# Two attention stages issued in another order, and the second rotary table's angles computed by GpSimd

## The reference

```python
# first block, per layer
y_mla  = mla_mixer(u_mla, ...)         # softmax attention, 4 heads, rotary angles of table 1
y_diff = diff_mixer(u_diff, ...)       # difference of two softmaxes, then rms_norm over the head
y_sb   = sb_mixer(u_sb)                # stick-breaking attention
mix = jnp.concatenate([y_mla, y_diff, y_sb], axis=-1) @ w_o[i]
h = layer_norm(DEEPNORM_ALPHA * h + mix, ln1_g[i], ln1_b[i])
# then 16 experts (grouped_moe) and a second layer_norm

# second block, per layer
a = gla_branch(gq, gk, gv, gg, glr, w_gate_up, b_gate, gla_norm_w) @ w_branch[0]
b = gmlp_branch(gz, gmlp_ln_g, gmlp_ln_b, gmlp_w_s, gmlp_b_s) @ w_branch[1]
c = moba_branch(mq, mk, mv, positions) @ w_branch[2]      # rotary angles of table 2
ga, gb, gc = jnp.split(jax.nn.sigmoid(gl), N_BRANCH, axis=-1)
x = layer_norm_2(x * alpha + (ga * a + gb * b + gc * c) @ w_out, ...)
```

## Time and profile before

| | before |
|---|---|
| median of three runs | 1705.57 us |
| the profiled execution, its own time | 1704.55 us |
| span of its instructions in the profile | 1703.3 us |
| PE busy | 1645.7 us (97%) |
| DVE busy | 890.1 us (52%) |
| ACT busy | 716.9 us (42%) |
| POOL busy | 33.0 us (2%) |

### The profile page before, as it was taken

One profiled execution on the slowest core, in us unless ns is written; L12 is line 12 of the kernel. 1 busy time (PEld: TensorE's weight loads), 2 busy tenths in 40 slices (PEclk: granted clock), 3 DMA queues, 4 the chain that ended last, 5 costly groups with the idle time before them and its releaser, 6 DMA issues.

```text
span 1703.3 us, 25713 instructions
## 1 busy us (share of the span) xinstructions
PE 1645.7 (97%) x10980; PEld 1287.6 (76%) x10980; DVE 890.1 (52%) x1174; ACT 716.9 (42%) x1078; POOL 33.0 (2%) x56
## 2 busy tenths in 40 slices
PE   8899999997999999998999999999999999999998
PEld 7778644434978744433989998899889899989997
DVE  7786411113587511113568556655566675675555
ACT  4685211112575311112654543544446454354443
POOL 1000000000000000000001000000000100000000
PEclk9999999999999999998999999999999999999999
DMA  9436999997736999998744555555556355546552
GB/s 282 153 130 219 373 418 416 416 417 267 239 116 223 373 417 416 416 417 311 234 149 149 174 193 178 198 186 185 177 174 198 119 179 168 203 141 230 186 185 75
DMA packets 193111, 413.11 MB, mean 243 GB/s; under 512 B 16416, under 2 KB 130848, under 8 KB 176608
## 3 DMA queue, kind: packets, MB, share of 16 engines
q1 hardware_dynamic: 191904, 409.81, 66.8%
q10 hardware_dynamic: 1088, 1.57, 0.4%
HBM read 409.52 MB, written 1.84 MB: 242 GB/s over the span
## 4 chain that ended last, share of the span: by engine, by line
PE 85%; DVE 8%; DMA 4%; ACT 2%; issue 1%; POOL 0%; SPq 0%; ACTq 0%; DVEq 0%
PE PS L1619 12%; PE PS L488 10%; PE PS L492 10%; PE PS L489 10%; PE PS L496 8%; PE PS L499 8%; PE PS L500 8%; PE PS L1641 6%; DMA arena<-in_w_up 2%; DVE weights_lo L468 2%; PE PS L1653 2%; PE PS L1594 2%; PE PS L515 2%; DMA weights_raw<-in_w_in 1%; DVE hT_lo L705 1%
## 5 line engine op out<-in xcount | busy, mean ns | idle before, releaser
L468 DVE TENSOR_TENSOR weights_lo<-weights_raw,weights_hi 128x1024 fp32r<-128x1024 f32 x368 | 431.1, 1216 | 189.3 <-ACT weights_hi L461 188.8
L461 ACT ACTIVATE weights_hi<-weights_raw 128x1024 fp32r<-128x1024 f32 x368 | 365.5, 1044 | 135.3 <-PE PS L500 70.5
L488 PE MATMUL PS<-hT_hi,weights_hi 128*128 128x256 f32 (+1 forms) x1456 | 411.2, 282 | 6.1 <-ACT bias L878 2.4
L492 PE MATMUL PS<-hT_hi,weights_lo 128*128 128x256 f32 (+1 forms) x1456 | 410.0, 282 | 1.9 <-DVE weights_lo L468 1.9
L489 PE MATMUL PS<-hT_lo,weights_hi 128*128 128x256 f32 (+1 forms) x1456 | 409.1, 281 | 0.0
L488 PEld LDWEIGHTS PS<-hT_hi,weights_hi 128*128 128x128 f32 (+1 forms) x1456 | 275.1, 189 | 10.6 <-issue 5.7
L492 PEld LDWEIGHTS PS<-hT_hi,weights_lo 128*128 128x128 f32 (+1 forms) x1456 | 274.9, 189 | 3.0 <-DVE weights_lo L468 2.7
L489 PEld LDWEIGHTS PS<-hT_lo,weights_hi 128*128 128x128 f32 (+1 forms) x1456 | 275.0, 189 | 1.3
L496 PE MATMUL PS<-weights_hi,opa_hi 128*128 128x512 f32 x384 | 153.5, 400 | 0.2
L500 PE MATMUL PS<-weights_hi,opa_lo 128*128 128x512 f32 x384 | 151.6, 395 | 0.0
L499 PE MATMUL PS<-weights_lo,opa_hi 128*128 128x512 f32 x384 | 151.5, 395 | 0.0
(11 more groups left out here) (318 smaller groups left out, 2332.2 us busy)
## 6 DMA issues: line engine op xcount, KB each, us to landing
weights_raw<-in_w_in SPq DMA_DIRECT2D x80, 1024.0 KB, 5.6
weights_raw<-in_w_ff SPq DMA_DIRECT2D x64, 1024.0 KB, 5.2
arena<-in_w_down SPq DMA_DIRECT2D x28, 1024.0 KB, 20.8
arena<-in_w_up SPq DMA_DIRECT2D x22, 1024.0 KB, 13.0
weights_raw<-in_w_gate SPq DMA_DIRECT2D x20, 1024.0 KB, 16.2
arena<-in_w_gate SPq DMA_DIRECT2D x18, 1024.0 KB, 17.5
weights_at_lo<-in_w_down SPq DMA_DIRECT2D x18, 1024.0 KB, 18.2
weights_at_hi<-in_w_up SPq DMA_DIRECT2D x18, 1024.0 KB, 16.2
```

The costliest lines, as they stand in the source:

```text
L461: act.activation(u.flat[0][:, c:e], u.x[:, c:e], ACT.Copy).then_inc(*sig.mark("w_hi", u.u, i))
L468: dve.tensor_tensor(u.flat[1][:, c:e], u.x[:, c:e], u.flat[0][:, c:e].bitcast(F32), ALU.subtract).then_inc(*sig.mark("w_lo", u.u, i))
L488: pe.matmul(o, w[0], x[0], start=start, stop=False)
L492: return pe.matmul(o, w[1], x[0], start=False, stop=stop)
```

## The change

Three things are done, apart from line numbers.

1. In the first block's attention, "sb y" comes ahead of "diff y" on PE, diff y goes to banks 6 and 7 instead of 3 and 4, and the output units come in the order 3, 1, 2, 0. ACT and DVE follow: ACT takes the exponential of the stick-breaking weights without splitting a unit ahead of it, DVE subtracts the cumulative sums before it looks at diff y's squares, and the third output unit is split later on both.
2. In the second block's mixer, "branch gate 000" comes ahead of the attention's scores, the softmax is interleaved with the first gates on ACT and DVE, and `feed("branch gate 100")` is moved ahead: on ACT ahead of the high part of gMLP's result, on DVE ahead of the two products of "branch 01".
3. In layer 0, DVE no longer computes the angles of table 2. GpSimd does, in 22 instructions and without fused operations, and ACT takes the four sines together, between bias steps 13 and 14.

```diff
-        for i in (1, 2, 3, 0):
+        for i in (3, 1, 2, 0):
...
-            if first:
-                for t in range(NT):
-                    banks.hold(pe, f"{label} t{t}", (4 + 2 * t, 5 + 2 * t), "dve_took")
...
+                    if not begun:
+                        banks.hold(pe, f"{label} t{t}", (4 + 2 * t, 5 + 2 * t), "dve_took")
...
-                    act.wait_ge(*sig.at("tab_dve", f"angle {blk}{part}"))
-                    act.activation(rope_tab[:, 2 * blk + part, :], red[part], ACT.Sin,
+                    act.wait_ge(*(sig.at("tab_pool", f"angle 1{part}") if blk else sig.at("tab_dve", f"angle 0{part}")))
+                    act.activation(rope_tab[:, 2 * blk + part, :], rope_tab[:, 2 + part, :] if blk else red[part], ACT.Sin,
...
                 if i == 13:
                     sines(0)
+                    sines(1)
                     yield
...
-            sines(1)
...
-                if blk:
-                    dve.wait_ge(*sig.at("tab_act", f"rope {blk - 1}"))
...
+        def angles_gpsimd(pool):
+            c = "tab_pool"
+            step(pool, c, pool.tensor_scalar(ang2, posf[:, 1, :], col(COL_INV1 + 1), None, ALU.mult))
+            for part in range(2):
+                r = rope_tab[:, 2 + part, :]
+                step(pool, c, pool.tensor_scalar(turns2, ang2, 1.0 / TWO_PI, 0.25 * (1 - part), ALU.mult, ALU.add))
+                step(pool, c, pool.tensor_scalar(turns2, turns2, MAGIC, None, ALU.add))
+                step(pool, c, pool.tensor_scalar(turns2, turns2, MAGIC, None, ALU.subtract))
+                for former, piece in ((ang2, PI1), (r, PI2), (r, PI3)):
+                    step(pool, c, pool.tensor_scalar(piece2, turns2, -piece, None, ALU.mult))
+                    step(pool, c, pool.tensor_tensor(r, former, piece2, ALU.add))
+                if part == 0:
+                    step(pool, c, pool.tensor_scalar(r, r, TWO_PI / 4, None, ALU.add))
+                step(pool, c, pool.tensor_scalar(r, r, 3.1415925, -3.1415925, ALU.min, ALU.max), f"angle 1{part}")
 
         def tables_tensor(pe):
...
                 scores(pe, n_(f"mla s{t}"), t, lambda hd, t, n: (qf[0:96, hd, t * P:(t + 1) * P], kf[0:96, hd, 0:n]),
                        at=(2, 0)[t])
-            pe.wait_ge(*sig.at("diff_dve", n_("rows")))
-            for t in range(NT):
-                b = banks.hold(pe, n_(f"diff y{t}"), (3 + t,), "act_took")
-                for hd in range(4):
-                    last = transpose(pe, PS[:, b, hd * P:(hd + 1) * P], orow1[:, t, hd, :])
-                last.then_inc(*sig.mark("ps", n_(f"diff y{t}")))
             pe.wait_ge(*sig.at("sb_act", n_("weights")))
             b = banks.hold(pe, n_("sb y"), (3,), "act_took dve_took")
             for hd in range(4):
                 last = values_T(pe, half_rows(b, hd), sv, z, hd)
             last.then_inc(*sig.mark("ps", n_("sb y")))
-
+            pe.wait_ge(*sig.at("diff_dve", n_("rows")))
+            for t in range(NT):
+                b = banks.hold(pe, n_(f"diff y{t}"), (6 + t,), "act_took")
+                for hd in range(4):
+                    last = transpose(pe, PS[:, b, hd * P:(hd + 1) * P], orow1[:, t, hd, :])
+                last.then_inc(*sig.mark("ps", n_(f"diff y{t}")))
+
+            pe.wait_ge(*sig.at("dve_took", n_("sb y")))
+            accumulate_rows(pe, L("w_o 3"), opa, 6, n_("ln1"), True, False)
             pe.wait_ge(*sig.at("diff_dve", n_("y lo 0")))
-            accumulate_rows(pe, L("w_o 1"), opa, 2, n_("ln1"), True, False,
+            accumulate_rows(pe, L("w_o 1"), opa, 2, n_("ln1"), False, False,
                             midway=lambda: pe.wait_ge(*sig.at("diff_dve", n_("y lo 1"))))
-            accumulate_rows(pe, L("w_o 2"), opa, 4, n_("ln1"), False, False)
             turn_probs(pe, n_("mla"), M1, (0, 2), sig.at("mla_dve", n_("mla s1") + " probs"))
...
-            accumulate_rows(pe, L("w_o 3"), opa, 6, n_("ln1"), False, False, midway=mla_y)
+            accumulate_rows(pe, L("w_o 2"), opa, 4, n_("ln1"), False, False, midway=mla_y)
...
-            feed(n_("w_o 1"))
...
             act.wait_ge(*sig.at("dve_took", n_("sb later")))
             act.activation(z, z, ACT.Exp).then_inc(*sig.mark("sb_act", n_("weights")))
+            act.wait_ge(*sig.at("ps", n_("sb y")))
+            hi_part(act, opa[0][:, 6:8, :], one_bank(banks.of(n_("sb y")), 2)).then_inc(*sig.mark("act_took", n_("sb y")))
             for t in range(NT):
                 act.wait_ge(*sig.at("ps", n_(f"diff y{t}")))
                 step(act, "act_took", act.activation(y_raw[t], one_bank(banks.of(n_(f"diff y{t}")), 4), ACT.Copy,
                                                      scale=b1cols[:, l, 3:4]), n_(f"diff y{t}"))
                 hi_part(act, opa[0][:, 2:6, t * P:(t + 1) * P], y_raw[t]).then_inc(*sig.mark("diff_act", n_(f"y hi {t}")))
+            feed(n_("w_o 3"))
             mla_exp(0)
-            act.wait_ge(*sig.at("ps", n_("sb y")))
-            hi_part(act, opa[0][:, 6:8, :], one_bank(banks.of(n_("sb y")), 2)).then_inc(*sig.mark("act_took", n_("sb y")))
             mla_exp(1)
-            feed(n_("w_o 2"))
+            feed(n_("w_o 1"))
             act.wait_ge(*sig.at("p_in", l))
...
-            dve.wait_ge(*sig.at("junk_act", n_("diff squares")))
-            dve.tensor_scalar(so1[:, 8:16], so1[:, 0:8], 1.0 / P, EPS_LN, ALU.mult, ALU.add).then_inc(*sig.mark(c, n_("diff var")))
...
                 zi = z[:, 2 * i:2 * i + 2, :]
                 dve.tensor_tensor(zi, zi, PS[:, 4 + 2 * i:6 + 2 * i, 0:384], ALU.subtract).then_inc(
                     *sig.mark("dve_took", n_("sb later")))
+            dve.wait_ge(*sig.at("junk_act", n_("diff squares")))
+            dve.tensor_scalar(so1[:, 8:16], so1[:, 0:8], 1.0 / P, EPS_LN, ALU.mult, ALU.add).then_inc(*sig.mark(c, n_("diff var")))
...
             dve.tensor_tensor(o8, o8, bcast_last(so1[:, 16:24], P), ALU.mult).then_inc(*sig.mark(c, n_("rows")))
-            feed(n_("w_o 1"))
+            dve.wait_ge(*sig.at("act_took", n_("sb y")))
+            lo_part(dve, opa[1][:, 6:8, :], one_bank(banks.of(n_("sb y")), 2), opa[0][:, 6:8, :]).then_inc(
+                *sig.mark("dve_took", n_("sb y")))
             mla_max(0)
             for t in range(NT):
                 s = slice(t * P, (t + 1) * P)
                 dve.wait_ge(*sig.at("diff_act", n_(f"y hi {t}")))
                 lo_part(dve, opa[1][:, 2:6, s], y_raw[t], opa[0][:, 2:6, s]).then_inc(*sig.mark(c, n_(f"y lo {t}")))
             mla_max(1)
+            feed(n_("w_o 3"))
             mla_probs(0)
-            dve.wait_ge(*sig.at("act_took", n_("sb y")))
-            lo_part(dve, opa[1][:, 6:8, :], one_bank(banks.of(n_("sb y")), 2), opa[0][:, 6:8, :]).then_inc(
-                *sig.mark("dve_took", n_("sb y")))
             mla_probs(1)
-            feed(n_("w_o 2"))
+            feed(n_("w_o 1"))
             turn_takes(dve, n_("mla"), 2, 1, MT, copy).then_inc(*sig.mark("dve_took", n_("mla") + " turn1"))
             dve.wait_ge(*sig.at("ple_act", n_("p hi")))
...
+            if l == 0:
+                angles_gpsimd(pool)
...
+                pe.wait_ge(*sig.at("mix_dve", n_("k rope")))
+                for t in range(NT):
+                    scores(pe, n_(f"mix s{t}"), t, lambda hd, t, n: (mq[:, hd, t * P:(t + 1) * P], mk[:, hd, 0:n]))
 
             def gate_and_branch(i):
                 for half in range(2):
-                    project_T(pe, L(f"branch gate {i}{half}0", f"branch gate {i}{half}1"), hT, "act_took")
+                    for j in range(2):
+                        project_T(pe, L(f"branch gate {i}{half}{j}"), hT, "act_took")
+                        if i == half == j == 0:
+                            mix_scores()
                 pe.wait_ge(*sig.at("opb_dve", n_(f"branch {i}")))
                 project_T_wide(pe, L(f"branch {i}0", f"branch {i}1"), opb, "dve_took", KC=4)
...
-                    project_takes(act, feed, L(f"branch gate {i}{half}0", f"branch gate {i}{half}1"), "act_took",
-                                  through(sigT[half], ACT.Sigmoid))
+                    for j in range(2):
+                        name = n_(f"branch gate {i}{half}{j}")
+                        if not (fed and half == j == 0):
+                            feed(name)
+                        act.wait_ge(*sig.at("ps", name))
+                        through(sigT[half], ACT.Sigmoid)(PS[:, banks.of(name), :].rearrange("p (j s) -> p j s", j=2), 2 * j).then_inc(
+                            *sig.mark("act_took", name))
+                        if i == half == 0:
+                            mix_exp(j)
                 feed(*L(f"branch {i}0", f"branch {i}1"))
 
             gate_and_branch(0)
+            feed(n_("branch gate 100"))
             act.wait_ge(*sig.at("ps", n_("branch 01")))
             act.wait_ge(*sig.at("gmlp_dve", n_("y")))
             hi_part(act, opb[0][:, :, :], zT).then_inc(*sig.mark("opb_act", n_("branch 1")))
```

(19 more changed lines are left out.)

23 lines of the change are left out of this document (9 added, 14 removed).

## The result

| | before | after |
|---|---|---|
| median of the runs compared (12 each) | 1703.53 us (1701.80 to 1705.96) | 1707.56 us (1705.40 to 1712.69) |
| ratio, 95% interval | | 1.0021 (1.0013 to 1.0029) |
| the profiled execution, its own time | 1704.55 us | 1709.4 us |
| span | 1703.3 us | 1708.2 us |

The changed kernel is 4.0 us slower, 0.21%, just at the bound of what can be told from no change. The interval of the ratio is +2.2 to +4.9 us, and I had forecast +0.5 us. Small as it is, the number is a sum of large terms of both signs.

A forecast was written before the change was run, and what follows sets the result against it. The prediction took the kernel as bound by PE, busy 1645.7 of 1703.3 us. Attention -7.2, mixer +6.2 and tables +1.5 gave +0.5 on the 1705.57 us median, so 1706.1 us; overall range 1700.5 to 1711.5.

The forecast's parts named there:

- R2: Mixer: clock stays at 1.2 GHz into the gates; mixer +9.4, sum +3.7 or more, 1709 to 1712 us; chance 0.2.
- the 0.15 us of another one: First block's attention: PE still waits some 0.15 us until DVE has the low part of sb y.
- R4: First block's attention: saving absent because probabilities or a load come late; up to +7 us, 1713 us; chance 0.05.
- T: Mixer: moment when PE ends "branch 01", 967.46 before and 965.9 forecast after; the delay is counted from it.
- 1.55: Mixer, each layer: PE runs branch gate 000 during its former wait for the rotated keys, saving 1.55 us.
- the half clock of the transposes: Mixer, behind the 4 us wait: 0.82 us of transposes become 1.4 at half clock, twice.
- Term (a): Tables: two more sines ahead of bias steps 14 and 15 on ACT make PE 0.85 us late.
- Term (c): Tables: GpSimd's 22 instructions slow DVE's two-input instructions, 17 at 0.19 us, making PE late; +2.3 us taken.
- Term (b): Tables: DVE, rid of 16 instructions, starts its first maximum 0.8 us earlier; -0.8 with Term (a) inside.
- R3: Tables: each of 17 DVE instructions waits for a whole GpSimd instruction; tables +5.3, sum +4.3, 1709.9 us; chance 0.1.

The follow-up runs named there:

- e2: Kernel before with only the mixer edits (scores behind the first gate, interleaved softmax, early split for branch gate 100): 1713.3 us, ratio 1.0051.
- e10: Kernel after with 34 unread transposes added on PE behind branch 01 in each mixer, into free bank 7: 1705.19 us, ratio 1.0000.
- e7: Kernel before with GpSimd making table 2's angles instead of DVE, but table 2's sines at their old place: 1703.94 us, ratio 1.0004.
- e5: Kernel after with the early split behind branch gate 100 undone on DVE alone, ACT still splitting early: 1703.53 us, ratio 1.0000.
- e9: Kernel after with 30 unread transposes added on PE behind branch 01 in each mixer, into bank 4: 1709.45 us, ratio 1.0020.
- e6: Kernel before with GpSimd's 22 angle instructions added, DVE still computing the angles that the sines read: 1707.64 us, ratio 1.0016.
- e3: Kernel before with only the table edits (GpSimd makes table 2's angles, four sines together): 1706.5 us, ratio 1.0011.
- e4: Kernel after with the split behind branch gate 100 put back late on ACT and DVE, scores still behind the first gate: 1697.63 us, ratio 0.9957.

## Why the prediction was right, and where its sizes were off

The path held: each of the three parts has the sign and, but for one bank in the second mixer, the waits that I had written down. The sizes held less well. That 1706.1 us was forecast and 1707.56 measured is partly luck, since the kernel before is 1703.53 in twelve runs and not 1705.57: the change itself is +4.0 where I had +0.5. That is the size that I gave to the rival R2 (+3.7 or more).

**Part 1: -7.2 said, -7.1 measured.** The left wait is 0.39 us ahead of diff y, and the 0.15 us of another one isn't there. The probabilities weren't late, no row with idle time stands between w_o's units, and R4 fell. The trace gives 3.4 us in layer 0: from the scores' end to the router it is shorter by that, the router starting at 163.63 for 164.39 although its stage began 2.6 us late.

**Part 2: +6.2 said, +8.9 measured.** The chain came as written. I put the gate at T + 8.2; in the first layer it starts at 970.93, and T is 966.99 - 4.29 = 962.70, so T + 8.23. Two things were missing from the sum. In the second layer the banks have gone round: "branch 01" has banks 4 and 5 there, and both are those of turn0, so the transposes wait for both products and not for one. That gives 4.89 us of waiting and T + 8.8, 0.6 us more. Against the former starts, 3.5 us behind T in both layers, and with 1.55 taken off, that is 3.15 and 3.75 us. And behind it the clock stayed low for 4 us of the gates, 2.2 us. 3.15 + 3.75 + 2.2 = 9.1 us. The mis-sized term is the clock in the gates: I had it in the bounds (+9.4) and in R2, and took the middle. R2 did happen, in one layer of two in the kernel after, and in both in e2, where the same sum gives 10.1 us, within the interval of its time (+6.5 to +10.7). So the sum is good to about 1 us only. e10 shows that about 3.6 us of part 2 are the clock, of which my sum had the half clock of the transposes.

**Part 3: +1.5 said, +2.1 measured, and two errors in it partly cancelled.** PE is 5.2 us late behind the bias, and I had 0.85 + 2.3 = 3.15. Term (a), the sines: 0.85 said, 0.7 read. Term (c), GpSimd: 2.3 said; PE is 2.9 us late at the last tile that it waits for, 44.58 for 41.65. The remaining 1.6 us are a term that I had put at nothing in the forecast: the clock behind the new waits near 43 us (0.65 from 44 to 48). At 49.65 PE makes the products that it made at 45.15 before, 4.5 us late, and no wait stands between. Timeline of PE before:

```profile
45.15 0.86 PE L980 MATMUL PS<-opb_hi,steps_and_slots 128*16 128x384 f32 x4
```

And after:

```profile
49.65 0.68 PE L991 MATMUL PS<-opb_hi,steps_and_slots 128*16 128x384 f32 x3
```

In e7, e5, e9 and e10, where the clock stayed at 1.00, PE is 2.1 to 2.5 us late at both places, which is the 2.3 of my term.

The working behind the 2.3 was less good than the number. DVE runs 27 instructions without a pause from 30 us on. Timeline of DVE before, the first and the last tile of them:

```profile
30.28 1.15 DVE L938 SCALAR_TENSOR_TENSOR opb_lo<-arena,const,small 128x256 fp32r<-128x256 f32 x2
...
42.94 1.14 DVE L938 SCALAR_TENSOR_TENSOR opb_lo<-arena,const,small 128x256 fp32r<-128x256 f32 x2
```

And after:

```profile
30.38 1.28 DVE L936 SCALAR_TENSOR_TENSOR opb_lo<-arena,const,small 128x256 fp32r<-128x256 f32 x2
...
43.30 1.14 DVE L936 SCALAR_TENSOR_TENSOR opb_lo<-arena,const,small 128x256 fp32r<-128x256 f32 x2
...
46.69 1.76 DVE L936 SCALAR_TENSOR_TENSOR opb_lo<-arena,const,small 128x256 fp32r<-128x256 f32 x2
```

They took 42.94 + 1.14 - 30.28 = 13.8 us, and now 18.1 us, 4.3 us longer. My 3.2 us, from 17 instructions at 0.19, belong to a shorter stretch, up to the tile at 39.89 before, which is at 43.30 now: 3.4 us late. So that number was near, but by luck. The groups of DVE's instructions between 29 and 52 us show what was slowed. Before:

```profile
L468 DVE TENSOR_TENSOR weights_lo<-weights_raw,weights_hi 128x1024 fp32r<-128x1024 f32 x4 | 4.7, 1221 | 1.4 <-ACT weights_hi L461 1.4
L938 DVE SCALAR_TENSOR_TENSOR opb_lo<-arena,const,small 128x256 fp32r<-128x256 f32 x5 | 2.4, 479 | 0.1
L915 DVE TENSOR_SCALAR arena<-arena 128x256 f32<-128x256 f32 x2 | 0.6, 289 | 0.0
L907 DVE TENSOR_SCALAR arena<-arena 128x256 f32<-128x256 f32 x1 | 0.3, 294 | 0.0
```

And after:

```profile
L468 DVE TENSOR_TENSOR weights_lo<-weights_raw,weights_hi 128x1024 fp32r<-128x1024 f32 x2 | 3.1, 1583 | 0.0
L936 DVE SCALAR_TENSOR_TENSOR opb_lo<-arena,const,small 128x256 fp32r<-128x256 f32 x5 | 3.0, 593 | 0.1
L913 DVE TENSOR_SCALAR arena<-arena 128x256 f32<-128x256 f32 x2 | 0.9, 454 | 0.0
L905 DVE TENSOR_SCALAR arena<-arena 128x256 f32<-128x256 f32 x1 | 0.8, 783 | 0.0
```

I had counted the instructions with two inputs in SBUF alone. Those with one input, L905 and L913, are slowed as well, from 0.29 to 0.78 and 0.45 us. I gave the long 128 x 1024 halves the same 0.19 as the short ones, where they lost 0.36 each. And from the wait at 31.57 to the tile that is ready at 40.95, the trace of the kernel before has 13 instructions with two inputs, not 17. From start to start, the six with one input account for 1.3 of the 3.2 us that this stretch grew, the two long halves for 0.75, and the eleven short ones with two inputs for 1.1, 0.1 each.

Term (b) I had at -1.65 (the -0.8 with (a) in it), from the step that the first maximum would wait for PE's scores. In the trace after it waits for the bias to land through DRAM, at 77.50 (in e5 and e9 it does wait for the scores, 1.16 and 1.18 us). Before, DVE was ready for it only at 74.89, while the same transfer, issued 5.2 us earlier (66.46 and 71.66 on ACT's queue), would have landed at about 72.3 (an estimate). So DVE's angles had been 2.6 us late, and this slack takes up 2.6 of the 5.2 us. That is the number seen at the attention, 5.2 - 2.6 = 2.6, and it is why e6, which keeps DVE's angles, gives nothing back.

R3, the port rule, gave +5.3 for part 3 and fell as I had priced it: not every DVE instruction waits. The rule of the Trainium skill ("SBUF — State Buffer", Who interferes with whom) is more careful than my use of it: whoever issues first holds the shared pair for the whole instruction, and the one-input `tensor_scalar` belongs to it too when it runs in a two-port mode. By that rule both engines should be slowed in turns, and this is what the trace has. POOL's timeline after:

```profile
33.40 1.11 POOL L977 TENSOR_SCALAR arena<-arena 128x256 f32<-128x256 f32 x1
...
37.44 1.71 POOL L977 TENSOR_SCALAR arena<-arena 128x256 f32<-128x256 f32 x1
...
41.44 0.46 POOL L981 TENSOR_SCALAR rope_tab<-rope_tab 128x256 f32<-128x256 f32 x1
```

One-input instructions of one size take 0.46 us at the shortest here and 1.71 beside DVE's long halves. DVE's L905, 0.49 us longer than before, is longer by about one of the shortest. That it is a lock and not a shared rate, and whether `tensor_scalar` ran in such a mode, no run here shows; the first is the page's statement.

## What to carry to other kernels

A prefetch moved ahead in program order must be checked against the buffer that it writes: if that buffer is freed by the very step that PE is finishing, everything queued behind the prefetch waits for that step, and the prefetch can't begin earlier anyway. Price a new wait on PE with the clock behind it, for each layer apart, since banks that go round give two layers different waits. Work moved to GpSimd isn't free because GpSimd is idle: count every DVE instruction beside it, those with one input too, and ask which later slack will take the delay up.

## What the runs showed of the hardware

- Added, useless transposes in waits of 4.3 and 4.9 us made the kernel some 3.6 us faster (1.0021 to 1.0000, uncertain by 2 us); the granted clock stayed at 1.00 there. In e9's second mixer the clock rose from 0.50 to 1.00 within the 42 transposes, at about 1418 us, when PE had run nothing else since 1408.
- Behind much the same wait the clock came back with the first gate in one mixer (0.95 in the window of the gate's start, 1.00 in the next) and 4 us later in the other. With the first mixer of e2 (0.50 and 0.70 behind its gate) these are three different lengths of one state, and I can't say what decides. Near 44 us it fell in three kernels of one code up to there (0.65 to 0.67 in the kernel after, e3 and e4, behind waits of 1.88, 1.78 and 1.56 us), and not in e5, e9 and e10 (1.27, 1.25 and 1.49 us).
- A DVE `tensor_scalar` of 128 x 256 with one input took 0.29 us alone and 0.42 to 0.78 beside GpSimd; GpSimd's own took 0.45 to 1.71.
